# Bias rearranged by GpSimd into reading order, and all turned probabilities copied from PSUM by ScalarE

## The chip, the cores and the metric

One core of one Trainium2 chip runs the whole program in one launch. The metric is the device time of that launch in microseconds (us), as a median over runs. Five engines work beside each other and meet only at semaphores: TensorE (PE in the profile, with PEld for its weight loads), VectorE (DVE), ScalarE (ACT), GpSimd (POOL) and SyncE (SP), which mostly issues transfers. Each takes its instructions in order.

## What is computed

The reference is a small network over 1024 tokens (a grid of 16 rows and 64 columns) and 256 context tokens, all in float32, width 1024. Two hybrid layers (a short convolution, a retention branch and a neighbourhood attention branch side by side) are followed by a block with a recurrent mixer, a pooling mixer and a feed-forward part. Only the neighbourhood attention matters here. For each of 6 heads of width 64, a query at grid place (r, c) looks at a window of 8 rows by 16 columns around it and at all 256 context tokens:

```
s_loc = einsum(q, k_win) * scale + rpb[head, dr, dc]     # a bias for each offset in the window
s_ctx = einsum(q, k_ctx) * scale                         # no bias
p = softmax(concat([s_loc, s_ctx]))
o = p_loc @ v_win + p_ctx @ v_ctx
```

In the first of the two layers the 256 context tokens also attend among themselves; in the second they don't.

## The kernel before

Nearly all the work is in dense products: a weight slab of 128 output features is loaded by SP into one of two buffers `raw[0]`, `raw[1]`, GpSimd splits it into a high and a low part (`split`, L480 and L482), and TensorE runs three matmuls for each product (`slab`, L561). Slabs are numbered; `split_done`, `slab_done` and `evac_done` count them. In each layer the slabs of the neighbourhood projections come first, then the stretch of this case, the attention itself, and then the slabs of the convolution (numbers from `G_CONV` on). Of those, the first two slabs have been loaded before the attention begins, and the second is still being split when it begins.

**The attention.** The queries are arranged so that a tile is 8 grid columns by 16 rows (128 queries), tiles t = 0 to 7. A tile sees three tiles of keys (24 columns by 16 rows, 384 keys) and the 256 context keys, 640 in all; keys are stored column by column, so a key's place is 16 * column + row. Heads go in pairs (j = 0, 1, 2). A unit is a (j, t), done in the order of `NA_ORDER`, and in the first layer two units of context queries follow in each pair (256 keys only): 30 units in the first layer, 24 in the second. A unit has these steps:

- scores (`scores`, L828): TensorE makes 128 x 640 scores for each of the two heads into PSUM banks 0 to 3 (matmuls on L846, L850 for context units). It first waits for `nm_ready` of the unit before.
- maxima (`maxima`, L1817): for each head VectorE adds the bias to the scores, writes the sum to `Sb`, takes the row maximum (L1839, one custom instruction) and negates it (L1841), which gives `nm_ready`. `Sb` has two buffers for head 0 and one for head 1, so head 1 waits until TensorE has turned the head 1 of the unit before.
- exponentials (`exps`, L1326): ScalarE, on `Sb` in place, with the row sum (L1331).
- turning (`turn_keys`, L854): TensorE transposes ten tiles of 128 x 128 into PSUM banks 4 to 6 (L867), 4, 4 and 2 to a bank (a context unit has four tiles, one bank). Head 1 begins with the sixth tile and waits for the exponentials of head 1.
- copies out of PSUM (`turned`): ScalarE copies banks 4 and 6 (L1342), VectorE copies bank 5 (L1856), into the single buffer `PT`, so each waits until the products of the unit before have been made.
- products (`apply`, L871): 20 matmuls of turned probabilities and values (L884) and 4 that spread the inverse sums (L888). VectorE multiplies them into `Y` (`place`, L1869 and L1870).

The engines run ahead of each other by one unit. The orders that matter are:

```
PE : scores(i+1)  turn_keys(i)  apply(i-1)
ACT: exps(i+1, head 0)  turned(i)  exps(i+1, head 1)
DVE: maxima(i+1)  sums(i)  turned(i)  place(i-1)
```

**The bias.** In HBM the bias is laid out row by row: a key's place is 64 * row + column. For each pair of heads three bias tiles are loaded: one for the middle tiles (t = 1 to 6), one for t = 0 and one for t = 7. `load_bias` (L389) issues eight transfers for one of them. There are two slots; a slot is two heads of 128 x 1024, and slot 1 is `biasB0` and the weight buffer `raw[0]`. `biases` (L439) issues the loads from SP, each as soon as `nm_ready` says that a slot is free; the first one of a layer is issued from ScalarE. The bias is read through a view in which neighbouring elements are 64 words apart, since scores and bias have different orders. Context keys have no bias; VectorE clears that part of the slot (L1822, L1823) at each switch. Behind the last bias load SP goes on with the weight slabs.

GpSimd does nothing in the attention stretch, other than finishing the split of the second convolution slab: its next split waits for the first convolution slab.

Of the kernel before, what the change touches and what calls it, by code (L numbers as in the profile page):

```python
# [114 lines left out]
NA_ORDER = [1, 2, 0, 3, 4, 7, 5, 6]  # L115
# [48 lines left out]
def build_kernel(nc, xT, cT, modw, vecs, mats, ropes, rets, bias, s8, s4, s2, rgw, poolw, pooltab, pT, outT):  # L164
    V, A, T, G = nc.vector, nc.scalar, nc.tensor, nc.gpsimd
    with ExitStack() as ctx:
# [39 lines left out]
        biasA = at("biasA", W_CT, [P, 2, SEQ])  # L206
        biasB0 = at("biasB0", W_B + 2 * NEAR_KEYS, [P, SEQ])
# [36 lines left out]
        bias_slot = [[biasA[:, 0, :], biasA[:, 1, :]], [biasB0[:], raw[0][:]]]  # L244
# [61 lines left out]
        bias_in = [sem("bias_in0"), sem("bias_in1")]  # L306
        s_ready, nm_ready = sem("s_ready"), sem("nm_ready")
        p_ready, pt_ready, pt_dve, pt_act = sem("p_ready"), sem("pt_ready"), sem("pt_dve"), sem("pt_act")
# [25 lines left out]
        CUTS = (0, 14, LAYER_AT[1] + 14, G_RMIX)  # L334
# [36 lines left out]
        def bias_tile(t):  # L371

            return t if t in (0, QT - 1) else 1

# [4 lines left out]
        def bias_loads(l, slot):  # L379

            return [(m, j, t) for m in range(l + 1) for j in range(PAIRS) for t in (1, 0, QT - 1)
                    if bias_slot_of(j, t) == slot]

        def bias_count(l, j, t):

            slot = bias_slot_of(j, t)
            return 128 * (bias_loads(l, slot).index((l, j, bias_tile(t))) + 1)

        def load_bias(eng, l, j, t):  # L389

            slot = bias_slot_of(j, t)
            for x, nx in BIAS_ROWS:
                k0 = 2 * min(max(x - 2, 0), QT - KEYT) * GRID_W
                b = (PAIRS * l + j) * QT + x
                r = 2 * BLK_W * x
                for a in range(2):
                    src = bias[b:b + nx, :, a, :].rearrange("x (y q) n -> (x y) q n", y=2)
                    eng.dma_start(bias_slot[slot][a][r:r + 2 * BLK_W * nx, k0:k0 + LOC],
                                  src[:, BLK_W * t:BLK_W * (t + 1), :]).then_inc(bias_in[slot], 16)
# [24 lines left out]
        def _(sp):  # L424
# [14 lines left out]
            def biases(l):  # L439

                units, ub = na_units(l), na_base(l)
                for j in range(PAIRS):
                    if j == 0:
                        sp.wait_ge(bias_clear, 2 * l + 2)
                    else:
                        sp.wait_ge(nm_ready, 2 * (ub + j * na_tiles(l)))
                    load_bias(sp, l, j, 0)
                    sp.wait_ge(nm_ready, 2 * (ub + units.index((j, 0)) + 1))
                    load_bias(sp, l, j, QT - 1)
                    sp.wait_ge(nm_ready, 2 * (ub + units.index((j, QT - 1)) + 1))  # L450
                    if j + 1 < PAIRS:
                        load_bias(sp, l, j + 1, 1)
# [20 lines left out]
        def _(pool):  # L473
# [27 lines left out]

            for g0, turns, places in runs(CUTS):
                if g0 == 0:
# [12 lines left out]
                if g0 + 2 * turns in CUTS[1:3]:  # L516
                    weighted_queries(CUTS.index(g0 + 2 * turns) - 1)

# [12 lines left out]
        def _(pe):  # L531
# [102 lines left out]
            for l in range(2):  # L634
# [193 lines left out]
                def scores(i):  # L828

                    j, t = units[i]  # L830
                    if i:
                        if i == 1:
                            keep_busy(7, 4)
                        pe.wait_ge(nm_ready, 2 * (ub + i))
# [19 lines left out]
                def turn_keys(i):  # L854
# [3 lines left out]
                    ga, gd = groups_before(l, i, 0, 2), groups_before(l, i, 1, 2)  # L858
                    for x, (a, _, p) in enumerate(tiles):
# [4 lines left out]
                        if x == 4 and gd:  # L864
                            pe.wait_ge(pt_dve, gd)
# [5 lines left out]
                def apply(i):  # L871
# [4 lines left out]
                    pe.wait_ge(pt_act, groups_before(l, i + 1, 0, 2))  # L876
                    pe.wait_ge(pt_dve, groups_before(l, i + 1, 1, 2))
# [294 lines left out]
        def _(act):  # L1172
# [35 lines left out]
            for l in range(2):  # L1208
# [105 lines left out]
                act.wait_ge(bias_clear, 2 * l + 1)  # L1314
                load_bias(act, l, 0, 1)
# [18 lines left out]
                def turned(i):  # L1334

                    for g in range(0, turned_groups(units[i][1]), 2):
# [1077 lines left out]
```

## Time and profile before

| | us |
|---|---|
| median of 3 runs | 3225.45 |
| lowest and highest | 3223.82, 3229.87 |
| the profiled execution's own time | 3228.54 |
| its span in the trace | 3226.7 |
| attention stretch, first layer | from 477.6 to 610 |
| attention stretch, second layer | from 1257.6 to 1372.6 |

| engine | busy us | share of the span |
|---|---|---|
| PE | 3120.1 | 97% |
| DVE | 1511.6 | 47% |
| ACT | 730.4 | 23% |
| POOL | 1131.6 | 35% |

Times inside the trace count from the start of the span. A row of the timeline gives the start, the length, the engine, the line of the kernel, the operation, what it writes and reads, how many instructions are merged in it, and in brackets how long the engine stood idle before it and for whom it waited. The ends of matmuls are modelled.

### The profile page before, as it was taken

The page shows a single profiled execution, that of the slowest core. Times are in us where ns is not written, and L with a number is a line of the kernel's source. Part 1 is how long each engine was busy: PE and PEld are TensorE (multiplying, and loading weights), DVE is VectorE, ACT ScalarE, POOL GpSimd, SP SyncE. Part 2 cuts the span into 40 slices and gives each one's busy share as a digit, 9 for nine tenths or more (in the row PEclk, how much of TensorE's full clock was granted, in tenths as well). Part 3 has the DMA queues.
Part 4 walks back from the last instruction along what each step waited for, and adds up shares of the span by engine and source line. Part 5 has one row for each costly group of instructions (what it writes and reads, how often), then busy time and mean ns, then how long its engine had stood idle before and what let it go on. Part 6 is the DMA issues. An engine that isn't in the chain of part 4 may idle for free.

```text
span 3226.7 us, 41362 instructions
## 1 busy us (share of the span) xinstructions
PE 3120.1 (97%) x17382; PEld 2527.6 (78%) x17382; DVE 1511.6 (47%) x1647; ACT 730.4 (23%) x940; POOL 1131.6 (35%) x525
## 2 busy tenths in 40 slices
PE   6999998899999999899999999999899999999998
PEld 5877886787878787788577788788688888888877
DVE  3124508428733423824677601443664056155477
ACT  2011215312231122511245501122211001001132
POOL 2222230026643222034133444453244344443442
PEclk9999999999999999999999999999999999999999
DMA  6200011333231011112111111112211111111211
GB/s 238 78 27 14 33 43 44 112 117 134 66 128 40 10 45 40 60 40 98 72 46 46 40 53 50 39 53 98 78 52 46 52 46 48 50 46 52 106 44 72
DMA packets 60188, 206.07 MB, mean 64 GB/s; under 512 B 5904, under 2 KB 7696, under 8 KB 60048
## 3 DMA queue, kind: packets, MB, share of 16 engines
q1 hardware_dynamic: 42384, 143.15, 13.7%
q10 hardware_dynamic: 17664, 60.87, 5.0%
q8 instruction: 111, 1.82, 0.2%
q14 instruction: 29, 0.24, 0.0%
HBM read 187.22 MB, written 16.78 MB: 63 GB/s over the span
## 4 chain that ended last, share of the span: by engine, by line
PE 77%; DVE 10%; issue 7%; POOL 3%; DMA 2%; ACT 1%; ACTq 0%; POOLq 0%; DVEq 0%; SPq 0%
PE ps L561 66%; DVE Sb L1839 3%; PE ps L846 2%; POOL w_hi L480 1%; POOL w_lo L482 1%; DVE C L2070 1%; DMA raw<-s 1%; PE ps L1034 1%; DMA modfirst<-modw 1%; PE ps L756 1%; PE ps L671 1%; PE ps L536 1%; PE ps L589 1%; PE ps L1015 0%; PE ps L762 0%
## 5 line engine op out<-in xcount | busy, mean ns | idle before, releaser
L480 POOL TENSOR_TENSOR w_hi<-raw,pool_zero 128x1024 fp32r<-128x1024 f32 (+2 forms) x242 | 457.6, 1891 | 2000.8 <-PE ps L561 1826.9
L482 POOL TENSOR_TENSOR w_lo<-raw,w_hi 128x1024 fp32r<-128x1024 f32 (+2 forms) x242 | 639.1, 2641 | 19.0
L561 PE MATMUL ps<-h_hi,w_hi 128*128 128x512 f32 (+1 forms) x1808 | 481.9, 363 | 6.2 <-POOL w_lo L482 2.5
L561 PE MATMUL ps<-g_hi,w_hi 128*128 128x512 f32 x1488 | 465.9, 394 | 2.1 <-DVE g_lo L2151 1.5
L561 PE MATMUL ps<-h_hi,w_lo 128*128 128x512 f32 (+1 forms) x1808 | 461.9, 352 | 0.0
L561 PE MATMUL ps<-h_lo,w_hi 128*128 128x512 f32 (+1 forms) x1808 | 461.5, 351 | 0.0
L561 PE MATMUL ps<-g_lo,w_hi 128*128 128x512 f32 x1488 | 459.1, 390 | 0.0
L561 PE MATMUL ps<-g_hi,w_lo 128*128 128x512 f32 x1488 | 459.1, 390 | 0.0
L561 PEld LDWEIGHTS ps<-h_hi,w_hi 128*128 128x128 f32 x1808 | 296.4, 188 | 76.5 <-issue 24.3
L561 PEld LDWEIGHTS ps<-h_hi,w_lo 128*128 128x128 f32 x1808 | 293.7, 188 | 48.9
L561 PEld LDWEIGHTS ps<-g_hi,w_hi 128*128 128x128 f32 x1488 | 279.4, 189 | 67.2 <-issue 7.0
L561 PEld LDWEIGHTS ps<-h_lo,w_hi 128*128 128x128 f32 x1808 | 293.3, 188 | 47.9
L561 PEld LDWEIGHTS ps<-g_lo,w_hi 128*128 128x128 f32 x1488 | 279.9, 188 | 58.6
L561 PEld LDWEIGHTS ps<-g_hi,w_lo 128*128 128x128 f32 x1488 | 279.9, 188 | 58.5
L561 PE MATMUL ps<-r_hi,w_lo 128*128 128x512 f32 x576 | 177.4, 389 | 0.0
L561 PE MATMUL ps<-r_hi,w_hi 128*128 128x512 f32 x576 | 177.3, 389 | 0.0
L561 PE MATMUL ps<-r_lo,w_hi 128*128 128x512 f32 x576 | 177.2, 389 | 0.0
L2195 DVE TENSOR_TENSOR gpad<-ps,token_scale 128x1024 f32<-128x1024 f32 x24 | 29.4, 1225 | 209.3 <-PE ps L561 201.2
L561 PEld LDWEIGHTS ps<-r_hi,w_hi 128*128 128x128 f32 x576 | 108.1, 188 | 22.5
L561 PEld LDWEIGHTS ps<-r_hi,w_lo 128*128 128x128 f32 x576 | 108.1, 188 | 22.4
L561 PEld LDWEIGHTS ps<-r_lo,w_hi 128*128 128x128 f32 x576 | 108.1, 188 | 22.4
L1585 ACT ACTIVATE ffc<-ffc,vec 128x1024 f32<-128x1024 f32 x24 | 27.6, 1152 | 342.4 <-DVE ffc L2200 342.4
(333 smaller groups left out, 3529.6 us busy)
## 6 DMA issues: line engine op xcount, KB each, us to landing
raw<-s SPq DMA_DIRECT2D x226, 512.0 KB, 3.5
modring<-modw ACTq DMA_DIRECT2D x32, 512.0 KB, 4.6
x_saved<-Y ACTq DMA_DIRECT2D x2, 4096.0 KB, 12.8
modfirst<-modw SPq DMA_DIRECT2D x4, 1024.0 KB, 10.7
modfirst<-modw ACTq DMA_DIRECT2D x4, 1024.0 KB, 19.4
xin<-x_saved ACTq DMA_DIRECT2D x1, 4096.0 KB, 13.4
B<-x_saved ACTq DMA_DIRECT2D x1, 4096.0 KB, 15.5
x_saved<-B ACTq DMA_DIRECT2D x1, 4096.0 KB, 11.7
```

The lines of the kernel that those rows point to most:

```text
L480: G.tensor_tensor(w_hi[s][:, :n], raw[s][:, :n], zero.to_broadcast([P, n]), ALU.add).then_inc(hi_done, 1)
L482: G.tensor_tensor(w_lo[s][:, :n], raw[s][:, :n], w_hi[s][:, :n].bitcast(F32), ALU.subtract)\
L536: T.matmul(ps[:, bank * BANK:bank * BANK + 3 * P].rearrange("p (x f) -> p x f", f=P), ones, cm[:], start=True, stop=True)
L561: last = T.matmul(ps[:, o + c0:o + c0 + size], wt[s][:, kk], xx[:, k, t0:t0 + size], start=(x == 0 and n == 0), stop=(x == k_n - 1 and n = ...
L589: last = T.matmul(ps[:, o + c0:o + c0 + size], wt[s][:, k * P:(k + 1) * P], xx[:, k, t0:t0 + size], start=(k == 0 and n == 0), stop=(k == ...
L671: last = T.matmul(ps[:, (6 + half) * BANK:(7 + half) * BANK], ret_const[:, 0, :], QK[:, c, CTX + 512 * half:CTX + 512 * (half + 1)], start ...
L756: T.matmul(ps[r, c:c + P], ST[r, d, STATE_AT[d](n), :], qw[i % 2][r, d, t * P:(t + 1) * P], start=(t == 0 and x == 0), stop=False, skip_gr ...
L846: last = T.matmul(ps[:, o:o + size], QK[r, 3 + j, q0:q0 + P], QK[r, j, k0:k0 + size], start=True, stop=True)
L1034: last = T.matmul(ps[:, (4 + 2 * m) * BANK + c0:(4 + 2 * m) * BANK + c0 + size], rgwt[:, 8 * m + c, :], xcs[c % 2][:, t0:t0 + size], start ...
L1839: own.link(V.tensor_tensor_reduce(out=p, in0=s, in1=b, scale=1.0, scalar=MASKED, op0=ALU.add, op1=ALU.max, accum_out=m[:, a:a + 1]))
L2070: ins = V.tensor_tensor(total, total, C2[:, 8 + k, :] if sq is None else sq, ALU.add)
L2195: V.tensor_tensor(gpad[:, 2:], ps[:, b:b + SEQ], token_scale[:], ALU.mult).then_inc(evac_done, 1)
```

## The change

- The bias tiles are now kept in reading order (16 * column + row, 640 words a head), in two slots of their own (`biasA` with three parts, and `biasB0`). The transfers go into a staging area instead: the first of a layer into `PT0` and `bias_raw0`, the other eight all into the pair `raw[0]`, `raw[1]`.
- GpSimd rearranges each tile from the staging area into its slot (`set_bias`): for each head a memset of 256 words and a copy of 384 words whose source elements are 64 words apart. Nine in each layer. It waits for the transfer and for the slot, and counts `bias_set`. The first of a layer stands ahead of the split of the first convolution slab; behind the split of the second one GpSimd sets both raw buffers to the masked value (`stage_clear`), and then does the other eight.
- SP issues the next bias load when `bias_set` says that the staging area has been read; before, it waited for a slot.
- VectorE waits for `bias_set` and reads the bias in one run of 640 words. Its memsets of the context part are gone. It also clears other areas ahead of the stretch (`PT0` and `bias_raw0`, 2048 words, in place of 4096).
- TensorE's scores wait for `s_read` of both heads, which VectorE's L1839 instruction counts itself, and not for the negated maximum that follows it.
- VectorE's copy of bank 5 is gone. ScalarE makes three copies (4, 4 and 2 tiles), and TensorE waits for all three where it waited for two of ScalarE and one of VectorE.
- The order of the tiles puts t = 0 fifth (third before) and t = 7 seventh (sixth before).
- The loops over slabs of GpSimd are cut at two more places in each layer, for the new calls.

```diff
-NA_ORDER = [1, 2, 0, 3, 4, 7, 5, 6]
+NA_ORDER = [1, 2, 3, 4, 0, 5, 7, 6]
...
-        biasA = at("biasA", W_CT, [P, 2, SEQ])
-        biasB0 = at("biasB0", W_B + 2 * NEAR_KEYS, [P, SEQ])
+        biasA = at("biasA", W_CT, [P, 3, NEAR_KEYS])
+        biasB0 = at("biasB0", W_B + 2 * NEAR_KEYS, [P, NEAR_KEYS])
+        bias_raw0 = at("bias_raw0", W_B, [P, SEQ])
...
-        bias_slot = [[biasA[:, 0, :], biasA[:, 1, :]], [biasB0[:], raw[0][:]]]
+        bias_slot = [[biasA[:, 0, :], biasA[:, 1, :]], [biasA[:, 2, :], biasB0[:]]]
+        bias_raw = [[PT0[:], bias_raw0[:]], [raw[0][:], raw[1][:]]]
...
-        CUTS = (0, 14, LAYER_AT[1] + 14, G_RMIX)
+        CUTS = (0, 14, G_CONV, G_CONV + 2, LAYER_AT[1] + 14, LAYER_AT[1] + G_CONV, LAYER_AT[1] + G_CONV + 2, G_RMIX)
...
+        bias_order = [(j, t) for j in range(PAIRS) for t in (1, 0, QT - 1)]
...
-                units, ub = na_units(l), na_base(l)
-                for j in range(PAIRS):
-                    if j == 0:
-                        sp.wait_ge(bias_clear, 2 * l + 2)
+                for n, (j, t) in enumerate(bias_order[1:]):
+                    if n == 0:
+                        sp.wait_ge(stage_clear, l + 1)
                     else:
-                        sp.wait_ge(nm_ready, 2 * (ub + j * na_tiles(l)))
-                    load_bias(sp, l, j, 0)
-                    sp.wait_ge(nm_ready, 2 * (ub + units.index((j, 0)) + 1))
-                    load_bias(sp, l, j, QT - 1)
-                    sp.wait_ge(nm_ready, 2 * (ub + units.index((j, QT - 1)) + 1))
-                    if j + 1 < PAIRS:
-                        load_bias(sp, l, j + 1, 1)
+                        sp.wait_ge(bias_set, 9 * l + n + 1)
+                    load_bias(sp, l, j, t, 1, stage_in)
+                sp.wait_ge(bias_set, 9 * (l + 1))
...
+            def set_bias(l, n):
+
+                j, t = bias_order[n]
+                units, ub = na_units(l), na_base(l)
+                if n:
+                    pool.wait_ge(stage_in, 128 * (8 * l + n))
+                else:
+                    pool.wait_ge(stage_first, 128 * (l + 1))
+                if t == QT - 1:
+                    pool.wait_ge(nm_ready, 2 * (ub + units.index((j, 0)) + 1))
+                elif j and t:
+                    pool.wait_ge(nm_ready, 2 * (ub + units.index((j - 1, QT - 1)) + 1))
+                elif j:
+                    pool.wait_ge(nm_ready, 2 * (ub + j * na_tiles(l)))
+                slot = bias_slot_of(j, t)
+                c0 = ROW if t == QT - 1 else 0
+                k0, z0 = (CTX, 0) if t == QT - 1 else (0, NEAR_KEYS - CTX)
+                for a in range(2):
+                    b = bias_slot[slot][a]
+                    G.memset(b[:, z0:z0 + CTX], 0.0)
+                    last = G.tensor_copy(b[:, k0:k0 + NEAR_KEYS - CTX].rearrange("p (c r) -> p c r", r=ROWS),
+                                         bias_raw[1 if n else 0][a].rearrange("p (r c) -> p c r", c=GRID_W)[:, c0:c0 + ROW_LOC, :])
+                last.then_inc(bias_set, 1)
+
             for g0, turns, places in runs(CUTS):
+                for l in range(2):
+                    if g0 == LAYER_AT[l] + G_CONV:
+                        set_bias(l, 0)
+                    if g0 == LAYER_AT[l] + G_CONV + 2:
+                        pool.wait_ge(split_done, g0)
+                        G.memset(raw[0][:], MASKED)
+                        G.memset(raw[1][:], MASKED).then_inc(stage_clear, 1)
+                        for n in range(1, 9):
+                            set_bias(l, n)
...
-                        pe.wait_ge(nm_ready, 2 * (ub + i))
+                        pe.wait_ge(s_read, 2 * (ub + i))
...
-                    ga, gd = groups_before(l, i, 0, 2), groups_before(l, i, 1, 2)
+                    ga = groups_before(l, i, 0, 1)
                     for x, (a, _, p) in enumerate(tiles):
                         if x == 0 or a != tiles[x - 1][0]:
                             pe.wait_ge(p_ready, 2 * (ub + i) + a + 1)
                         if x == 0 and ga:
                             pe.wait_ge(pt_act, ga)
-                        if x == 4 and gd:
-                            pe.wait_ge(pt_dve, gd)
...
-                    pe.wait_ge(pt_act, groups_before(l, i + 1, 0, 2))
-                    pe.wait_ge(pt_dve, groups_before(l, i + 1, 1, 2))
+                    pe.wait_ge(pt_act, groups_before(l, i + 1, 0, 1))
...
-                act.wait_ge(bias_clear, 2 * l + 1)
-                load_bias(act, l, 0, 1)
+                act.wait_ge(bias_clear, l + 1)
+                load_bias(act, l, 0, 1, 0, stage_first)
...
-                    for g in range(0, turned_groups(units[i][1]), 2):
-                        n = 4 if g == 0 else 2
+                    for g in range(turned_groups(units[i][1])):
+                        n = 2 if g == 2 else 4
...
-                V.memset(biasA[:], MASKED).then_inc(bias_clear, 1)
-                V.memset(biasB0[:], MASKED)
-                dve.wait_ge(split_done, g0 + G_CONV + 1)
-                V.memset(raw[0][:], MASKED).then_inc(bias_clear, 1)
+                V.memset(PT0[:], MASKED)
+                V.memset(bias_raw0[:], MASKED).then_inc(bias_clear, 1)
                 units, ub = na_units(l), na_base(l)
-
-                def zeros(j, t, a):
-
-                    return bias_slot[bias_slot_of(j, t)][a].rearrange("p (r c) -> p r c", c=GRID_W)[:, :, ROW_LOC:ROW]
 
                 def maxima(i):
 
                     j, t = units[i]
                     if t in (0, 1, QT - 1):
-                        dve.wait_ge(bias_in[bias_slot_of(j, t)], bias_count(l, j, t))
-                        V.memset(zeros(j, t, 0), 0.0)
-                        own.link(V.memset(zeros(j, t, 1), 0.0))
+                        dve.wait_ge(bias_set, 9 * l + bias_order.index((j, t)) + 1)
                     dve.wait_ge(s_ready, ub + i + 1)
                     m = st[:, i % 2, :]
                     for a in range(2):
@@ -1829,15 +1836,12 @@
                         elif i >= 2:
                             dve.wait_ge(pt_ready, groups_before(l, i - 1, 0, 1))
                         size, o = NEAR_KEYS if t < QT else CTX, 2 * a * BANK
-                        if t < QT:
-                            c0 = ROW_LOC if t == QT - 1 else 0
-                            b = bias_slot[bias_slot_of(j, t)][a].rearrange("p (r c) -> p c r", c=GRID_W)[:, c0:c0 + ROW, :]
-                        else:
-                            b = zeros(j, 1, a)
-                        p, s = [x.rearrange("p (c r) -> p c r", r=ROWS) for x in (probabilities(i, a)[:, :size],
-                                                                                  ps[:, o:o + size])]
-                        own.link(V.tensor_tensor_reduce(out=p, in0=s, in1=b, scale=1.0, scalar=MASKED, op0=ALU.add,
-                                                        op1=ALU.max, accum_out=m[:, a:a + 1]))
+                        b = bias_slot[bias_slot_of(j, t if t < QT else 1)][a]
+                        b = b if t < QT else b[:, NEAR_KEYS - CTX:]
+                        p, s = probabilities(i, a)[:, :size], ps[:, o:o + size]
+                        V.tensor_tensor_reduce(out=p, in0=s, in1=b, scale=1.0, scalar=MASKED, op0=ALU.add,
+                                               op1=ALU.max, accum_out=m[:, a:a + 1]).then_inc(s_read, 1)
+                        dve.wait_ge(s_read, 2 * (ub + i) + a + 1)
                         V.tensor_scalar(m[:, 2 + a:3 + a], m[:, a:a + 1], -1.0, None, ALU.mult).then_inc(nm_ready, 1)
 
                 def sums(i):
@@ -1846,14 +1850,6 @@
                     if i >= 2:
                         dve.wait_ge(pv_ready, ub + i - 1)
                     V.reciprocal(st[:, i % 2, 6:8], st[:, i % 2, 4:6]).then_inc(rinv_ready, 1)
-
-                def turned(i):
-
-                    if units[i][1] < QT:
-                        dve.wait_ge(pt_ready, groups_before(l, i, 0, 1) + 2)
-                        if ub + i:
-                            dve.wait_ge(pv_ready, ub + i)
-                        V.tensor_copy(turned_tile(4, 4), ps[:, 5 * BANK:6 * BANK]).then_inc(pt_dve, 1)
 
...
-                    turned(i)
```

## Rows read from the trace of the kernel before

**Rows 1.** The page, part 4: shares of the chain that ended last, by line.

```profile
PE ps L561 66%; DVE Sb L1839 3%; PE ps L846 2%; POOL w_hi L480 1%; POOL w_lo L482 1%; DVE C L2070 1%; DMA raw<-s 1%; PE ps L1034 1%; DMA modfirst<-modw 1%; PE ps L756 1%; PE ps L671 1%; PE ps L536 1%; PE ps L589 1%; PE ps L1015 0%; PE ps L762 0%
```

**Rows 2.** Timeline, VectorE: head 0 of units 1, 27 (first layer), 1, 23 (second).

```profile
483.46 1.27 DVE L1839 CUSTOM_DVE_ANT_1 Sb<-ps,biasA 128x640 f32<-128x640 f32 x1 [1.46 <-PE ps L846]
...
595.43 1.28 DVE L1839 CUSTOM_DVE_ANT_1 Sb<-ps,biasA 128x640 f32<-128x640 f32 x1 [0.22 <-PE ps L846]
...
1263.47 1.27 DVE L1839 CUSTOM_DVE_ANT_1 Sb<-ps,biasA 128x640 f32<-128x640 f32 x1 [1.46 <-PE ps L846]
...
1362.18 1.26 DVE L1839 CUSTOM_DVE_ANT_1 Sb<-ps,biasA 128x640 f32<-128x640 f32 x1 [0.22 <-PE ps L846]
```

**Rows 3.** Timeline of one unit in the first layer.

```profile
494.90 0.87 ACT L1342 ACTIVATE PT<-ps 128x512 f32<-128x512 f32 x2 [0.34 <-PE ps L888]
...
495.04 1.36 PE L846 MATMUL ps<-QK 64*128 64x384 f32 x12 [0.25 <-DVE st L1841]
...
495.65 0.83 ACT L1331 ACTIVATE Sb<-Sb,st 128x640 f32<-128x640 f32 x1
...
496.33 1.31 PE L867 MATMUL ps<-cm,Sb 128*128 128x128 f32 x10
...
496.45 1.27 DVE L1839 CUSTOM_DVE_ANT_1 Sb<-ps,biasA 128x640 f32<-128x640 f32 x1 [0.22 <-PE ps L846]
...
497.58 1.31 PE L884 MATMUL ps<-PT,Vt 128*64 128x128 f32 x20
...
497.83 1.28 DVE L1839 CUSTOM_DVE_ANT_1 Sb<-ps,biasA 128x640 f32<-128x640 f32 x1
...
498.72 0.39 PE L888 MATMUL ps<-cm,st 128*64 128x128 f32 x4
...
499.34 0.69 DVE L1856 COPY PT<-ps 128x512 f32<-128x512 f32 x1
...
499.37 1.35 PE L846 MATMUL ps<-QK 64*128 64x256 f32 x12 [0.26 <-DVE st L1841]
```

**Rows 4.** Timeline, end of the second layer's stretch: units without new scores.

```profile
1364.94 0.87 ACT L1342 ACTIVATE PT<-ps 128x512 f32<-128x512 f32 x2 [0.34 <-PE ps L888]
...
1365.70 0.83 ACT L1331 ACTIVATE Sb<-Sb,st 128x640 f32<-128x640 f32 x1
...
1366.67 0.53 PEld L867 LDWEIGHTS ps<-cm,Sb 128*128 128x128 f32 x5 [0.21 <-ACT Sb L1331]
...
1367.37 1.31 PE L884 MATMUL ps<-PT,Vt 128*64 128x128 f32 x20
...
1368.51 0.39 PE L888 MATMUL ps<-cm,st 128*64 128x128 f32 x4
...
1369.00 0.87 ACT L1342 ACTIVATE PT<-ps 128x512 f32<-128x512 f32 x2 [2.38 <-PE ps L888]
```

**Rows 5.** Groups by form, ScalarE, 477.6 to 610: copies of turned probabilities.

```profile
L1342 ACT ACTIVATE PT<-ps 128x512 f32<-128x512 f32 x30 | 17.8, 592 | 13.5 <-PE ps L888 13.5
...
L1342 ACT ACTIVATE PT<-ps 128x256 f32<-128x256 f32 x24 | 9.0, 377 | 0.0
```

**Rows 6.** Groups by form, VectorE, 477.6 to 610: bias, scores and maximum.

```profile
L1839 DVE CUSTOM_DVE_ANT_1 Sb<-ps,biasA 128x640 f32<-128x640 f32 x28 | 35.5, 1270 | 14.9 <-PE ps L846 14.7 <-DVE biasA L1823 0.2
...
L1839 DVE CUSTOM_DVE_ANT_1 Sb<-ps,biasA 128x256 f32<-128x256 f32 x8 | 3.4, 420 | 1.6 <-PE ps L867 1.3
```

**Rows 7.** Timelines, SyncE and VectorE, first layer: a bias load and its first reader.

```profile
575.89 0.71 SPq L398 DMA_DIRECT2D biasB<-bias  x1
...
586.22 0.27 DVE L1822 MEMSET biasB<- 128x256 f32 x1 [0.46 <-DMA raw<-bias]
```

**Rows 8.** GpSimd: timeline at the second stretch's start; then groups by form.

```profile
1258.58 2.36 POOL L482 TENSOR_TENSOR w_lo<-raw,w_hi 128x1024 fp32r<-128x1024 f32 x1
...
L480 POOL TENSOR_TENSOR w_hi<-raw,pool_zero 128x1024 fp32r<-128x1024 f32 x226 | 442.7, 1959 | 1918.5 <-PE ps L561 1744.6 <-PE ps L589 149.9 <-DMA raw<-s 24.0
...
L498 POOL TENSOR_TENSOR qw<-QK,WQ 128x384 f32<-128x384 f32 x12 | 11.7, 1000 | 17.2 <-PE ps L762 17.2
```

More of the change, by code:

```diff
@@ L304, in build_kernel @@
                                                             sem("hn_var"), sem("hn_std"), sem("hn_done"))
-        bias_in = [sem("bias_in0"), sem("bias_in1")]
-        s_ready, nm_ready = sem("s_ready"), sem("nm_ready")
-        p_ready, pt_ready, pt_dve, pt_act = sem("p_ready"), sem("pt_ready"), sem("pt_dve"), sem("pt_act")
+        stage_first, stage_in, stage_clear, bias_set = sem("stage_first"), sem("stage_in"), sem("stage_clear"), sem("bias_set")
+        s_ready, s_read, nm_ready = sem("s_ready"), sem("s_read"), sem("nm_ready")
+        p_ready, pt_ready, pt_act = sem("p_ready"), sem("pt_ready"), sem("pt_act")
         rinv_ready, pv_ready, y_used = sem("rinv_ready"), sem("pv_ready"), sem("y_used")
@@ L369, in groups_before, with load_bias @@
             return sum(len(range(first, turned_groups(t), step)) for _, t in done)
-        def bias_tile(t):
-            return t if t in (0, QT - 1) else 1
         def bias_slot_of(j, t):
             return (j + (t in (0, QT - 1))) % 2
[L379 to L391, printed above, removed]
+        bias_order = [(j, t) for j in range(PAIRS) for t in (1, 0, QT - 1)]
+        def load_bias(eng, l, j, t, place, landed):
             for x, nx in BIAS_ROWS:
@@ L397, in load_bias @@
                     src = bias[b:b + nx, :, a, :].rearrange("x (y q) n -> (x y) q n", y=2)
-                    eng.dma_start(bias_slot[slot][a][r:r + 2 * BLK_W * nx, k0:k0 + LOC],
-                                  src[:, BLK_W * t:BLK_W * (t + 1), :]).then_inc(bias_in[slot], 16)
+                    eng.dma_start(bias_raw[place][a][r:r + 2 * BLK_W * nx, k0:k0 + LOC],
+                                  src[:, BLK_W * t:BLK_W * (t + 1), :]).then_inc(landed, 16)
         def probabilities(i, a):
@@ L515, in _ @@
                         split(x % 2, k, g)
-                if g0 + 2 * turns in CUTS[1:3]:
-                    weighted_queries(CUTS.index(g0 + 2 * turns) - 1)
+                for l in range(2):
+                    if g0 + 2 * turns == LAYER_AT[l] + 14:
+                        weighted_queries(l)
         FULL = [(0, 0, 512), (512, 512, 512), (1024, 1024, 256)]
```

## The prediction, made before the changed kernel was run

> **What bounds the kernel now.** I read the chain of waits first: two thirds of it are TensorE's slab matmuls (L561), which the change leaves alone [rows 1]. The share that can move lies in the two attention stretches (L1839, L846). So I read those as a pipeline with one period a unit. From head 0 of unit 1 to head 0 of unit 23 the second layer takes 98.7 us for 22 steps, 4.49 a unit; the first takes 112.0 for 26, which at 4.49 for its 20 steps between local units leaves 3.7 for each of the 6 around context units [rows 2].
>
> One unit in detail [rows 3]: scores start at 495.04 and again at 499.37, a period of 4.33. VectorE's sums for head 0 start 1.41 after the scores (496.45), head 1's at 497.83, and the next scores follow 1.54 later. This is a closed ring: scores, two sums, scores. TensorE stands idle in it for only 0.26, so its own work is 4.07 a unit. The rest of the 4.49 is switches of the bias. ScalarE has room.
>
> **Each part of the change.**
>
> *VectorE's sum.* The strided bias is the likely price of the long form: 640 elements take 1.270 us, and 256, whose bias comes in short runs of neighbours, take 0.420 [rows 6]. Per element that is 1.98 and 1.64 ns with all fixed cost in it. No row has 640 in reading order. Below it is bounded by VectorE's copy of 512 out of PSUM, 0.69 [rows 3], above by today's 1.27; I take 0.82, on the line through 0.420 for 256 and 0.69 for 512. Two sums save 0.9 of the ring. `s_read` in place of `nm_ready` saves another 0.15 (the negation). The copy (0.69) and the memsets (0.27 each, as in [rows 7], 18 of each head) leave VectorE as well. So this ring falls to about 3.3 and is no longer what binds.
>
> *ScalarE's third copy.* The two copies start at 494.90 and the exponential of head 1, queued behind them, at 495.65 [rows 3]. Two take 0.87 together, one of 256 takes 0.377 [rows 5], so a copy of 512 holds the queue for 0.50. Now the ring that this lengthens: `turned(i)`, then head 1 of `exps(i+1)`, then the second half of `turn_keys(i+1)`, then `apply(i)`, and only then `turned(i+1)`, because `PT` has one buffer. At the end of the second stretch no scores stand between and the ring can be seen bare [rows 4]: copies at 1364.94, exponential 1365.70 (+0.76), second half of the turning 1366.67 (+0.97, released by the exponential), products 1367.37 (+0.70), inverse sums 1368.51 (+1.14), next copies 1369.00 (+0.49). That is 4.06. Today it hides under 4.33. With one more copy of 512 it is **4.56**, above TensorE's 4.07 and above today's period. The scores fit inside it: they start behind the inverse sums and take 1.29 (495.04 to 496.33), while the turning can't start before the third copy ends, some 1.5 after the first began.
>
> Against 4.49 this adds 0.07 a step: 22 steps give +1.6 in the second layer, 20 give +1.5 in the first (steps around context units have as many short copies as before: +0). The first scores of each layer come 1.0 sooner behind two short sums (-1.0 each). The last two rounds have a third copy each, with nothing to absorb it: +1.0 in the second layer, +0.5 in the first, where context units end it.
>
> *The bias through one staging area.* This is what I think costs most. Loads and rearrangements now alternate, since SP waits for `bias_set` and GpSimd for the load. A load takes 10.3 from its first issue (575.89) to the reader that waited for it (586.22) [rows 7]; two other waits of this kind give 10.2 and 10.8. A rearrangement is 2 memsets of 256 and 2 strided copies of 384. GpSimd has no such row. The nearest is its two-input product of 384 at 1.00 [rows 8]; I take 1.0 for the copy (one input less, but strided) and 0.3 for the memset (VectorE's takes 0.27), so 2.7 with a hand-over. Below: 0.55 and 0.27, VectorE's speed, 1.6 in all. Above: 1.5 and 0.5, 4.0. So one bias needs 10.3 + 2.7 + 0.1 = 13.1. Eight follow each other, and a pair of heads needs three, 39.3, while it lasts 8 x 4.56 = 36.5 in the second layer. The staging falls behind.
>
> In the second layer: the split ends at 1260.94 [rows 8], two memsets of 1024 (1.1 each; at most 1.96 as the split's first half) clear the staging at 1263.1, so biases n = 1 to 8 are set at 1276.2 + 13.1(n - 1). Units need them (units 4, 6, 8, 12, 14, 16, 20, 22) at 1262.5 + 4.56(k - 1). Late by: 0, 4.0, 8.0, 2.8, 6.8, 10.8, 5.7, 9.6. The largest counts once: 10.8. Some is absorbed: head 0 could start 1.2 after the copies and is needed by ScalarE 1.3 later than it comes, head 1 must let the scores go 1.1 later; take 1.1. Delay 9.7. Sum of the second layer: -1.0 + 1.6 + 9.7 + 1.0 = **+11.3**.
>
> In the first layer I take the split to end as far ahead of unit 1 (2.5). Bias 2 is set at 509.3, unit 6 wants it at 505.3: 4.0 less 1.1 is 2.9. After that a pair lasts 7 x 4.56 + 3 x 3.7 = 43.0, longer than 39.3, so nothing more. Sum: -1.0 + 1.5 + 2.9 + 0.5 = **+3.9**.
>
> *What costs nothing.* The first `set_bias` of a layer (2.7) stands where GpSimd waits some 7 us or more for TensorE in each round of splits. Weight slabs behind the last bias load: bias 8 is set at 1367.9 or later, the stretch ends near 1384, and the first convolution slab, already split, runs before they are wanted; if GpSimd were 10 us later still, this cover would be gone. VectorE's clearing is shorter than before.
>
> The page "GPSIMD Engine Reference" of the Trainium skill, Engine selection, says of GpSimd that one-input work is roughly line-rate, which would make 384 elements an estimated 0.3 us and the sum about +5. The same page's Performance pitfalls says that a read step over 8 bytes costs about 2.9 cycles an element, an estimated 0.9; no row here shows either.
>
> **Sum.** +11.3 + 3.9 = +15.2. The profiled execution took 3228.5, so it would take 3243.7; the median before is 3225.45, 3.1 lower, and on it I forecast **3241**.
>
> **Rivals.**
>
> A, the forecast (ring of 4.56 and staging of 13.1): 3241, chance 0.48.
>
> B, GpSimd slow (4.0 a bias, memsets of 1.96): staging 14.4; bias 8 is set at 1380.0 against 1358.3, delay 20.6, the second layer +22.2; the first waits 7.2 to 7.5, +8.5. Together +31: 3256, 0.15. Strided reads speak for it, no row against it.
>
> C, GpSimd fast (1.6 a bias): staging 12.0; the largest lateness is 4.5, less 1.1 is 3.4; second layer +5.0, first +1.5. +6.5: 3232, 0.12. The nearest row speaks against it. The line rate of the Trainium skill (page "GPSIMD Engine Reference", Engine selection) would lie here or lower.
>
> D, the third copy doesn't lengthen the period (4.33 stays), staging decides: unit 22 wants its bias at 1353.4, it comes at 1367.9, delay 13.4; second layer -1.0 - 3.4 + 13.4 = +9.0, first -1.0 - 3.2 + 4.0 = -0.2. +9: 3234, 0.11. Against it: the bare ring of [rows 4].
>
> E, **faster**: the copy is hidden, TensorE's 4.07 binds, and GpSimd takes 1.6. Then bias 8 (1358.9) is 10.9 later than unit 22 wants it (1348.0), delay 9.8; second layer -1.0 - 9.2 + 9.8 = -0.4, first -1.0 - 8.4 + 2.9 = -6.5. -7: 3218.5, 0.07. It decides from the point where copies, exponential, half turning and products fit in 4.07; ScalarE copies 512 in 0.592 where VectorE needs 0.69 [rows 3, 5], which speaks for it. "Advanced Engine Details and Errata" of the Trainium skill, TRN2 Errata, says the same, that ScalarE is closer to PSUM; by that rule alone the move is a gain.
>
> F, the change doesn't do what it says, sums stay at 1.27: head 1 then holds the scores back by 0.06 a unit, the first scores gain nothing, most of it vanishes under the staging. +17: 3242.5, 0.07.
>
> **How the numbers follow.** A measurement of this kernel tells about 0.2%, 6.5 us, from no change. Slower by more: A, B, D, F and half of C, 0.87, of which I give 0.05 to what I haven't seen: 0.82. Faster: E, 0.07. The rest, 0.11, is the same. The range leaves out E and the upper half of B: 3230 to 3258.
>
> **What would show it.** A period of 4.56 between units that wait for no bias, and ScalarE's three copies starting 0.50 apart, right behind L888. The second half of the turning released by ScalarE. VectorE's long form near 0.82. VectorE idle for GpSimd's copy at units 6, 8 and 16 of the second layer, about 3, 4 and 3 us, and once in the first. SP's loads 13 apart. If the waits for GpSimd are missing, the staging step is wrong; if the period is 4.1, the ring is; if GpSimd's copy takes 2 us, B it is.

## The result and the profile after

The changed kernel takes 3233.09 us (median of 9 runs) against 3225.45 before (the median of 9 runs too): 7.6 us slower, ratio 1.0021 with a 95% interval of 1.0012 to 1.0029. One of the nine, at a mean granted clock of 0.749, took 3926 us and is left out of the ratio. The direction is as forecast and the time lies in the range, but the increase is half of the 15.2 that the forecast added up.

In the trace the loss lies where it was expected, in the two attention stretches, from the first scores to the first matmul of the convolution slabs. Timeline of TensorE after the change, both ends of both stretches:

```profile
476.89 1.36 PE L864 MATMUL ps<-QK 64*128 64x384 f32 x12 [1.33 <-ACT Y L1194]
...
610.90 0.50 PE L579 MATMUL ps<-h_hi,w_hi 128*128 128x512 f32 x1 [0.71 <-DVE Y L1866]
...
1258.08 0.59 PE L864 MATMUL ps<-QK 64*128 64x384 f32 x2 [1.11 <-ACT Y L1194]
...
1378.49 0.38 PE L579 MATMUL ps<-h_hi,w_hi 128*128 128x256 f32 x1 [0.72 <-DVE Y L1866]
```

That is 134.0 and 120.4; before, the same ends stood at 477.63 and 610.45 (132.8) and 1257.64 and 1372.61 (115.0). So +1.2 and +5.4, 6.6 in all. The spans of the two profiled executions differ by only 4.6 (3231.3 and 3226.7): outside the stretches the second execution took 2.0 less. So a few us between medians or spans say less than the stretches do.

One unit of the first layer after the change, timeline (answers to [rows 3], and with its ring laid open to [rows 4]):

```profile
497.90 1.36 ACT L1357 ACTIVATE PT<-ps 128x512 f32<-128x512 f32 x3 [1.25 <-PE ps L903]
...
499.13 0.82 DVE L1842 CUSTOM_DVE_ANT_0 Sb<-ps,biasA 128x640 f32<-128x640 f32 x1 [0.67 <-PE ps L864]
499.13 0.84 ACT L1346 ACTIVATE Sb<-Sb,st 128x640 f32<-128x640 f32 x1
...
499.40 1.48 PE L883 MATMUL ps<-cm,Sb 128*128 128x128 f32 x10 [0.32 <-ACT PT L1357]
...
500.11 0.53 PEld L883 LDWEIGHTS ps<-cm,Sb 128*128 128x128 f32 x5 [0.21 <-ACT Sb L1346]
...
500.81 1.31 PE L899 MATMUL ps<-PT,Vt 128*64 128x128 f32 x20
...
501.95 0.39 PE L903 MATMUL ps<-cm,st 128*64 128x128 f32 x4
...
502.45 1.36 ACT L1357 ACTIVATE PT<-ps 128x512 f32<-128x512 f32 x3 [1.34 <-PE ps L903]
```

The three copies start at 497.90 and again at 502.45: a period of 4.55, where 4.56 had been worked out. Each link is there: the start of the three copies, then head 1's exponential (+1.23), the second half of the turning released by it (+0.98), products (+0.70), inverse sums (+1.14), copies (+0.50). TensorE, which stood idle 0.26 a unit before, now waits for the copies (0.32), and its weight loads for the exponential (0.21). VectorE's sum has the price that was forecast, and VectorE waits for TensorE (0.67) instead of setting the pace. Its group by form in the first stretch, which answers to [rows 6]:

```profile
L1842 DVE CUSTOM_DVE_ANT_0 Sb<-ps,biasA 128x640 f32<-128x640 f32 x38 | 31.3, 824 | 111.4 <-PE ps L864 100.9 <-PE ps L883 7.2 <-POOL biasB L506 3.4
```

824 ns against 1270 before: reading the bias in one run is worth 0.45 a sum.

The staging, GpSimd and SyncE in the first layer (answers to [rows 7] and to the unknown price beside [rows 8]):

```profile
492.17 0.31 POOL L505 MEMSET biasA<- 128x256 f32 x1 [9.87 <-DMA raw<-bias]
492.43 0.85 POOL L506 COPY biasA<-raw 128x384 f32<-128x384 f32 x1
...
493.47 0.86 POOL L506 COPY biasB<-raw 128x384 f32<-128x384 f32 x1
...
494.36 5.78 SPq L387 DMA_DIRECT2D raw<-bias  x8
...
504.18 0.31 POOL L505 MEMSET biasA<- 128x256 f32 x1 [9.85 <-DMA raw<-bias]
```

A rearrangement takes 2.2 (492.17 to 494.33) and not 2.7, a load 9.8 (494.36 to 504.18) and not 10.3. From one bias to the next it is 12.0, in place of 13.1. The next two views are the places where VectorE waits for it in the second layer, the sums of head 0 for units 6 to 10, and the granted clock of TensorE in windows around them (columns as on the page: window, PE, PEld, DVE, ACT, POOL busy, clock, transfers):

```profile
1287.16 0.82 DVE L1842 CUSTOM_DVE_ANT_0 Sb<-ps,biasA 128x640 f32<-128x640 f32 x1 [2.98 <-POOL biasB L506]
...
1290.39 0.82 DVE L1842 CUSTOM_DVE_ANT_0 Sb<-ps,biasA 128x640 f32<-128x640 f32 x1 [0.67 <-PE ps L864]
...
1298.76 0.82 DVE L1842 CUSTOM_DVE_ANT_0 Sb<-ps,biasA 128x640 f32<-128x640 f32 x1 [4.63 <-POOL biasB L506]
...
1301.99 0.82 DVE L1842 CUSTOM_DVE_ANT_0 Sb<-ps,biasA 128x640 f32<-128x640 f32 x1 [0.67 <-PE ps L864]
...
1307.76 0.82 DVE L1842 CUSTOM_DVE_ANT_0 Sb<-ps,biasA 128x640 f32<-128x640 f32 x1 [0.67 <-PE ps L864]
```

```profile
1295.00:1300.00 5.00, 2.94 (x34) 2.35 (x34) 1.20 (x4) 0.93 (x3) 2.13 (x4) 1.00 0.04 15
1300.00:1303.00 3.00, 2.23 (x16) 1.81 (x17) 2.23 (x9) 2.79 (x7) 0.00 (x0) 0.83 0.30 86
1303.00:1306.00 3.00, 3.00 (x28) 2.67 (x28) 1.09 (x5) 0.92 (x2) 0.00 (x0) 0.60 0.23 81
```

Three things are to be seen. Units 6 and 8 wait for GpSimd, as forecast, by 3.0 and 4.6 (in the first layer unit 6 does, by 3.4). The unit behind each wait follows after 3.23, not 4.55: 1.3 of it is made good at once. And behind the longer wait, in which TensorE stood idle for 2.6, its granted clock, 1.00 before (2.4 GHz), has means of 0.83 and 0.60 in the next two windows, so for a part of them it was at 1.2 GHz, and one unit took 5.77, 1.2 more than 4.55.

### The profile page after: what moved, and what is told of

Same layout as the page of the kernel before. It is cut to its first block, busy times and chain, and to the rows that moved or that the text cites. A ratio compares the mean times of both kernels' runs of the same rounds, so it can differ in the third digit from the quotient of the medians.

```text
span 3231.3 us, 41364 instructions
## 1 busy us (share of the span) xinstructions
PE 3126.9 (97%) x17382; PEld 2526.9 (78%) x17382; DVE 1435.1 (44%) x1561; ACT 753.7 (23%) x988; POOL 1173.3 (36%) x601
## 4 chain that ended last, share of the span: by engine, by line
PE 78%; issue 7%; DVE 6%; POOL 4%; DMA 2%; ACT 2%; SPq 1%; ACTq 0%; POOLq 0%; DVEq 0%
PE ps L579 66%; POOL w_hi L464 2%; POOL w_lo L466 1%; PE ps L883 1%; ACT PT L1357 1%; PE ps L899 1%; DVE C L2065 1%; PE ps L1049 1%; DMA raw<-s 1%; DMA modfirst<-modw 1%; PE ps L774 1%; PE ps L689 1%; SPq L387 1%; PE ps L554 1%; DMA raw<-bias 1%
## 5 line engine op out<-in xcount | busy, mean ns | idle before, releaser
L1842 DVE CUSTOM_DVE_ANT_0 Sb<-ps,biasA 128x640 f32<-128x640 f32 (+1 forms) x86 | 66.9, 778 | 222.9 <-PE ps L864 189.2
## 6 DMA issues: line engine op xcount, KB each, us to landing
xin<-x_saved ACTq DMA_DIRECT2D x1, 4096.0 KB, 12.8
```

The lines of the kernel that those rows point to most:

```text
L1842: V.tensor_tensor_reduce(out=p, in0=s, in1=b, scale=1.0, scalar=MASKED, op0=ALU.add, op1=ALU.max, accum_out=m[:, a:a + 1]).then_inc(s_read, 1)
```

## Experiments

The theory: (1) the third copy lengthens the ring to 4.55, and (2) the staging makes units wait in both layers. The rival to the first is that the copy is hidden and all of the loss is staging. Lengths of the two stretches, read in each trace from the same two rows as above:

| kernel | first | second | both, against before | median us | ratio to before (95%) |
|---|---|---|---|---|---|
| before | 132.8 | 115.0 | | 3225.45 | |
| changed | 134.0 | 120.4 | +6.6 | 3233.09 | 1.0021 (1.0012 to 1.0029) |
| copy_back | 125.0 | 115.6 | -7.3 | 3221.2 | 0.9986 (0.9977 to 0.9995) |
| direct | 133.1 | 115.7 | +1.1 | 3230.32 | 1.0011 (1.0002 to 1.0021) |
| both | 121.6 | 105.1 | -21.1 | 3205.65 | 0.9945 (0.9931 to 0.9958) |
| only_copies | 138.7 | 116.7 | +7.6 | 3233.1 | 1.0018 (1.0009 to 1.0027) |
| slow_set | 138.0 | 125.4 | +15.6 | 3242.17 | 1.0048 (1.0034 to 1.0062) |
| exp_first | 138.0 | 120.9 | +11.1 | 3239.66 | 1.0041 (1.0027 to 1.0055) |
| old_order | 143.0 | 124.5 | +19.7 | 3247.58 | 1.006 (1.0046 to 1.0074) |

The kernel before and the changed one were measured in a first batch, the others in two later ones, beside which the kernel before had medians of 3225.99 (first four) and 3226.39 (last three).

**copy_back.** The changed kernel, with VectorE's copy of bank 5 again.

```diff
-                    for g in range(turned_groups(units[i][1])):
-                        n = 2 if g == 2 else 4
+                    for g in range(0, turned_groups(units[i][1]), 2):
+                        n = 4 if g == 0 else 2
...
+                        V.tensor_copy(turned_tile(4, 4), ps[:, 5 * BANK:6 * BANK]).then_inc(pt_dve, 1)
```

> The changed kernel with one part undone: VectorE copies bank 5 of the turned probabilities again, ScalarE copies banks 4 and 6. Theory 1 (the third copy lengthens the ring of copies, exponential of head 1, turning, products to 4.55 us): a unit that waits for nothing takes about 4.1, TensorE's own 4.07; the first layer's stretch gets 8 us shorter than in the changed kernel, the second, where GpSimd and the transfers now set the pace (12.0 a bias, 36 for a pair against 32.8), only 5. Total near 3220, 5 below the kernel before. Theory 2 (the third copy is hidden and all of the loss is waiting for the staged bias): the period stays near 4.5 and the time near 3233.

Measured: 3221.2, and stretches 9.0 and 4.8 shorter than the changed kernel's, against 8 and 5 expected. The sums of head 0 in VectorE's timeline, units 11 and 15 of the second layer, and the waits in that layer:

```profile
1302.67 0.82 DVE L1845 CUSTOM_DVE_ANT_0 Sb<-ps,biasA 128x640 f32<-128x640 f32 x1
...
1318.93 0.83 DVE L1845 CUSTOM_DVE_ANT_0 Sb<-ps,biasA 128x640 f32<-128x640 f32 x1
```

```profile
POOL biasA L505 <- DMA raw<-bias: 79.4, 8, 10.4
...
DVE Sb L1845 <- POOL biasB L506: 10.1, 4, 4.5
DVE Sb L1845 <- POOL biasA L506: 2.7, 1, 2.7
```

Four units take 16.26 here, 4.07 each, and VectorE now waits for GpSimd five times in the second layer, 12.8 in all, where the changed kernel waited 8.5 (the two waits above and 0.9 at unit 16): the faster the units, the more the staging binds. Beside the staging the third copy costs about 12 us (3233.1 against 3221.2), so the theory that it is hidden falls. Without it the rest of the change gains some 5 us.

**direct.** No staging: the host lays the three tiles of a pair out in reading order, with their zeros (layout only, as it did before in another order), and SyncE brings each into its slot when `nm_ready` has freed it.

```diff
-            for x, nx in BIAS_ROWS:
...
+            for a in range(2):
+                eng.dma_start(bias_slot[slot][a], bias[n, :, a, :]).then_inc(bias_in[slot], 16)
...
-                        for n in range(1, 9):
-                            set_bias(l, n)
```

> The changed kernel with the staging gone: the host lays out the three bias tiles of a pair in reading order with the zeros of the context keys, two transfers bring one straight into its slot, GpSimd takes no part, ScalarE still makes three copies. Theory 1: the period stays 4.55, the waits of VectorE for GpSimd (3.4 in the first layer, 7.6 in the second, of which a good 1 each is absorbed) go: about 6 to 7 us less than the changed kernel, near 3226.5, the same as before. Theory 2 (staging alone costs): it falls to 4.1 a unit and to 3208.

Measured: by the stretches 0.9 and 4.7 below the changed kernel, 5.6 in all, a little less than the 6 to 7 expected. The median of 3230.3 is only 2.8 lower, and 4 above the 3226.5 expected; the profiled execution took 3227.3, 3 below that median. So the size lies between 2.8 and 5.6, and what the difference is isn't settled. VectorE, head 0 of units 7 and 11 of the second layer:

```profile
1284.73 0.82 DVE L1811 CUSTOM_DVE_ANT_0 Sb<-ps,biasA 128x640 f32<-128x640 f32 x1 [0.67 <-PE ps L834]
...
1302.95 0.82 DVE L1811 CUSTOM_DVE_ANT_0 Sb<-ps,biasA 128x640 f32<-128x640 f32 x1 [0.67 <-PE ps L834]
```

The period is still 4.55 (18.22 for four units) with no staging at all, which is what theory 1 says and theory 2 of this run (4.1) doesn't.

**both.** The two edits together: of the change only the bias in reading order in slots of its own (without VectorE's memsets for it), the new release of the scores and the tile order are left. These are not told apart by any run.

> Staging gone and bank 5 back on VectorE, so that only the bias in reading order remains of the change. Theory 1: neither ring binds, TensorE's own work does, 4.07 to 4.1 a unit for 42 steps between local units: 22 x (4.49 - 4.1) + 20 x 0.39 = 16 below the kernel before and a little more for switches: 3208. Rival: something else near 4.33 binds (the wait of head 1 for the turning of the unit before), and it is near 3219.

Measured: 3205.65, 20 us and 0.55% below the kernel before, a little more than expected. VectorE, head 0 of three units in the second layer, and a window of four units (columns as above):

```profile
1300.67 0.82 DVE L1814 CUSTOM_DVE_ANT_0 Sb<-ps,biasA 128x640 f32<-128x640 f32 x1
...
1304.65 0.82 DVE L1814 CUSTOM_DVE_ANT_0 Sb<-ps,biasA 128x640 f32<-128x640 f32 x1
...
1308.81 0.82 DVE L1814 CUSTOM_DVE_ANT_0 Sb<-ps,biasA 128x640 f32<-128x640 f32 x1
...
1292.55:1308.81 16.26, 16.26 (x186) 13.19 (x185) 12.98 (x41) 10.40 (x25) 0.00 (x0) 1.00 0.31 91
```

Two units in 8.14, 4.07 each, which is TensorE's own work in [rows 3], and TensorE is busy for all of the 16.26 of the window. Nothing else binds here. This is the version to keep.

The four kernels with the new sum show that the two costs overlap. The third copy costs 24.7 without the staging (direct against both) and 11.9 with it; the staging costs 15.6 without the third copy (copy_back against both) and 2.8 with it (the changed kernel against direct). A slower unit asks for its bias later, and VectorE's waits for GpSimd fit this: 17.6 in copy_back, 11.9 in the changed kernel. Neither price can be read from one experiment alone.

**only_copies.** The kernel before with `turned` as in the change and nothing else.

> The kernel before with one part of the change: ScalarE makes all three copies, the bias and everything else as before (strided sums of 1.27 us). Theory 1: 4.55 a unit in place of 4.33, but the switches of the bias, 0.5 each, now hide below it: +0.07 to +0.15 for 42 steps and 1.5 at the ends: +4.5 to +8, 3230 to 3233. Theory 2 (the third copy is hidden, VectorE is relieved of 0.69): 4.33 stays or less, 3220 to 3225.

Measured: 3233.1, the upper end of theory 1. VectorE, head 0 of two units in the first layer:

```profile
505.58 1.28 DVE L1836 CUSTOM_DVE_ANT_1 Sb<-ps,biasA 128x640 f32<-128x640 f32 x1 [0.86 <-PE ps L846]
...
510.14 1.29 DVE L1836 CUSTOM_DVE_ANT_1 Sb<-ps,biasA 128x640 f32<-128x640 f32 x1 [0.86 <-PE ps L846]
```

4.56 a unit, with VectorE relieved of its 0.69 and idle for 0.86 where it was idle for 0.22. Moving the copy alone is a loss, and the same ring shows it with the strided sums of before. (The profiled execution was 5 us above its median. TensorE's granted clock had a mean of 0.66 from 570 to 575, where one unit took 5.31, and of 0.94 and 0.50 in the windows from 610 and from 615. So 138.7 is too long for this kernel, by 1 to 2 us; the rest of the 5 isn't explained.)

**slow_set.** The changed kernel with its staging slowed to what the forecast had assumed.

```diff
+                    G.memset(b[:, k0:k0 + NEAR_KEYS - CTX], 0.0).then_inc(extra, 1)
+                    pool.wait_ge(extra, 2 * (9 * l + n) + a + 1)
                     G.memset(b[:, z0:z0 + CTX], 0.0)
```

> The changed kernel, with one more memset of 384 words and a wait for it ahead of each half of a rearrangement, which puts a bias near 13.1 us in place of 12.0: the value that I had forecast. If the size of the staging was what the forecast had wrong, this kernel gives the forecast's sum: bias 6 of the second layer comes 6 x 1.05 later, that layer +6.3, the first one +2.1 (bias 2), 8 above the changed kernel, 3241. If the error lay elsewhere (slack, ends, early units), it gives 3237 or less.

Measured: 3242.17, 9.1 above the changed kernel. From one bias to the next it now takes 13.0:

```profile
1277.07 0.42 POOL L505 MEMSET biasA<- 128x384 f32 x1 [10.50 <-DMA raw<-bias]
...
1367.83 0.42 POOL L505 MEMSET biasA<- 128x384 f32 x1 [9.61 <-DMA raw<-bias]
```

Seven steps in 90.8. With the forecast's input the kernel gives nearly the forecast's output, 3242 for 3241, and by stretch +5.2 and +10.4 for +3.9 and +11.3. So the size of this step is what separates 15 from 7. That the sum comes out within 1 us is partly luck: windows of this trace hold 13.6 us at half clock (6.8 in each layer) where those of the changed kernel hold 3.4, a cost that the forecast didn't have. One us in a step that eight biases go through one after the other costs 9 us.

**exp_first.** The kernel direct, with ScalarE's order turned round.

```diff
-                    turned(i)
                     if i + 1 < len(units):
                         exps(i + 1, 1)
+                    turned(i)
```

> The kernel without staging and with three copies by ScalarE, in which ScalarE makes the exponential of head 1 ahead of the copies and not behind them. If the ring is what I say, taking the exponential out of it doesn't help, because the sum of head 1 waits for the turning of the unit before and the copies now wait for it: turning, sum of head 1 (1.2), exponential (0.95), copies (1.5): about 4.7 a unit in place of 4.55, +6 us, 3236. If ScalarE's order is of no account, the time stays near 3230.

Measured: 3239.66, 9.3 above direct (10.0 by the stretches), where 6 was expected. Head 0 of units 4 and 6 of the second layer starts at 1278.51 and 1287.88 and of unit 20 at 1353.45: 74.9 for 16 units, 4.68 a unit, as worked out (4.7). That gives 5.5 for 42 steps. Of the rest, 3 lie in the units behind the start of a stretch or, in the first layer, of a pair (unit 3 of the second layer takes 5.14 for direct's 4.11) and 1.4 behind the last sums; why isn't settled. The order that the kernel has is the better one.

**old_order.** The changed kernel with the tile order of before.

> The changed kernel with the tile order of before, so that the staged biases are wanted at units 2 and 5 of the first pair, not at 4 and 6. Bias 1 is set at 1275.3 in the second layer, unit 2 wants it at 1267: 7 us of delay in place of 4 to 5 in the second layer and 2 in the first: about 6 us above the changed kernel, 3239. If the order is of no account, 3233.

Measured: 3247.58, 14.5 above the changed kernel, where 6 was expected. The wait stands where it was expected, at unit 2, but it costs more. VectorE, units 1 and 2 of the first layer, windows behind them, and TensorE's turning of one unit:

```profile
482.37 0.82 DVE L1842 CUSTOM_DVE_ANT_0 Sb<-ps,biasA 128x640 f32<-128x640 f32 x1 [1.99 <-PE ps L864]
...
494.51 0.82 DVE L1842 CUSTOM_DVE_ANT_0 Sb<-ps,biasA 128x640 f32<-128x640 f32 x1 [9.81 <-POOL biasB L506]
```

```profile
490.00:495.00 5.00, 0.00 (x0) 0.00 (x0) 0.49 (x1) 0.00 (x0) 2.09 (x4) 0.68 0.06 23
495.00:500.00 5.00, 3.67 (x18) 2.85 (x19) 2.92 (x12) 3.03 (x8) 0.00 (x0) 0.50 0.18 57
500.00:505.00 5.00, 4.67 (x45) 3.75 (x44) 2.27 (x7) 2.69 (x6) 0.55 (x2) 0.80 0.20 74
```

```profile
498.76 2.39 PE L883 MATMUL ps<-cm,Sb 128*128 128x128 f32 x10
```

TensorE does nothing in the window from 490 to 495, and its granted clock is at half from within it until after 500; turning takes 2.39 where it takes 1.48. So the new tile order is a part of the change that pays for itself, given the staging: it moves the first use of bias 1 from unit 2 to unit 4.

## Why the prediction was right and where it was wrong

The terms of the forecast's sum against the stretches, each stretch cut at head 0 of its unit 1 and of its last local unit (27 and 23), in us against the kernel before:

| | forecast | changed | direct |
|---|---|---|---|
| first layer, up to unit 1 | -1.0 | -0.35 | -0.35 |
| first layer, steps and waits | +1.5 and +2.9 | 0.0 | -0.9 |
| first layer, end | +0.5 | +1.5 | +1.5 |
| second layer, up to unit 1 | -1.0 | -0.4 | -0.35 |
| second layer, steps and waits | +1.6 and +9.7 | +4.7 | 0.0 |
| second layer, end | +1.0 | +1.1 | +1.1 |
| sum | +15.2 | +6.6 | +1.1 |

*What binds before.* The ring of scores and sums at 4.33 with TensorE's 4.07 below it: both shows TensorE's 4.07 once that ring is gone. Right.

*VectorE's sum, 0.82.* Measured 0.824. Right, and right too that it gains nothing while another ring is longer: with three copies and no staging (direct) the stretches are where they were.

*The third copy, 4.56.* Measured 4.55, and 4.56 with the old sums (only_copies). As a period it is right to the last link. But the forecast put it into all 42 steps between local units, +3.1, and direct, which has this ring and no staging, shows -0.9 and 0.0: behind the start of a stretch, and behind the context units, it isn't reached yet (in the second layer of direct units 2 and 3 follow after 3.53 and 4.11, in the first layer the units behind the context units after 3.23, 3.53 and 4.36). This term is 4.0 too high. What the copy costs depends on what else binds: 24.7 where nothing does (direct against both), 11.9 beside the staging (the changed kernel against copy_back), 7 beside the old sums (only_copies against before).

*The first scores 1.0 sooner.* From the first scores to the first sum of unit 1 it was 5.83 before (477.63 to 483.46) and is 5.48 now (476.89 to 482.37): 0.35. The filler matmuls that TensorE runs ahead of the scores of unit 1 (`keep_busy(7, 4)`, 478.18 to 480.96) now hold them back, which I hadn't counted. The end of the first layer costs 1.5 where I put 0.5.

*The staging, 13.1.* **This is the term that was mis-sized.** It is 12.0: the copy of 384 takes 0.85 where I put 1.0, from a two-input row; the two heads follow each other without a gap; the load takes 9.8 where I put 10.3. The mechanism was right (units 6 and 8, and a wait of 0.9 at unit 16 of the second layer; unit 6 of the first). But the delay is a small difference of two long rows of steps: with 12.0 in place of 13.1, and nothing else changed in the forecast's own working, the largest lateness is that of unit 8, 4.7 less 1.1, so 3.6 in place of 9.7, and in the first layer 1.8 less 1.1, 0.7 in place of 2.9. Measured, as changed less direct, the waits cost 4.7 and 0.9, and 1.2 of the 4.7 is the unit of 5.77 at the lower clock. slow_set, which puts the 13 back, makes 3242. With 12.0 the forecast's sum would be +6.9, near the 6.6 of the stretches, and there luck helps: the steps are 4.0 too high in it, the starts and ends together 2.4 too low and the waits 1.3.

*The slack of 1.1.* Measured 1.3 (3.23 in place of 4.55 behind a wait).

*The rivals.* The nearest number was rival C's, 3232, with a staging of 12.0. Its 12.0 was made of a rearrangement of 1.6 and a load of 10.3, where 2.2 and 9.8 were measured: the sum is right because the two errors cancel. D and E fall with the period of 4.55, F with the sum of 0.82, and B with a copy of 0.85.

The estimate of 0.9 for a strided copy of 384, worked out from the page "GPSIMD Engine Reference" of the Trainium skill, Performance pitfalls, was nearer to the 0.85 of the trace than the 1.0 from my row. The same page's line rate (Engine selection), an estimated 0.3, doesn't hold for this copy. With "Advanced Engine Details and Errata" of the Trainium skill, TRN2 Errata, which puts ScalarE closer to PSUM, the measured copies agree, 0.59 on ScalarE and 0.69 on VectorE; but the move was a loss, because it was ScalarE's place in the ring that counted and not the price of the copy.

## What to carry to other kernels

Before moving work to the engine that is less busy, follow what is queued behind it and close the ring: here ScalarE was busy for 56% of the first stretch before the change (72.5 of 130.4 us), and 0.50 more on it lengthened the period, since its copies stood between two steps of TensorE. And where a buffer is filled, rearranged and read in turns, multiply its step by the number of turns before comparing it with the work beside it: 1 us in the step was 9 us in the end. Data that is reordered on the chip in every run can be laid out so once, on the host: here the staging cost 15.6 us in the version where nothing hid it.

## What the runs showed of the hardware that wasn't expected

A wait for a buffer can be paid for twice, the second time by the granted clock. Behind the TensorE idle of 2.6 us in the changed kernel the windows above hold 3.4 us at half clock (twice the length of a window times what its mean lacks to 1.00: 2 x 3 x 0.17 and 2 x 3 x 0.40), and the timeline has the turning of that unit at 2.37 where it takes 1.48:

```profile
1300.58 1.36 PE L864 MATMUL ps<-QK 64*128 64x384 f32 x12 [2.56 <-DVE st L1842]
1302.13 2.37 PE L883 MATMUL ps<-cm,Sb 128*128 128x128 f32 x10 [0.19 <-ACT PT L1357]
```

Behind the first-layer wait of old_order the windows hold 10.2. VectorE's waits for GpSimd there add up to 20.9 against 11.9 in the changed kernel, 9.0 more, and the time is 14.5 more. But the length of the idle time doesn't decide it alone. In copy_back TensorE stood idle for 3.16 and went on at full clock; in only_copies the clock fell behind an idle of 1.62, with no long wait for a bias near it. TensorE's scores behind the idle time, copy_back and then only_copies, and the windows there:

```profile
1279.86 1.36 PE L864 MATMUL ps<-QK 64*128 64x384 f32 x12 [3.16 <-DVE st L1845]
...
1280.00:1285.00 5.00, 5.00 (x58) 4.02 (x58) 4.19 (x14) 3.48 (x10) 0.00 (x0) 1.00 0.25 87
```

```profile
569.81 2.38 PE L846 MATMUL ps<-QK 64*128 64x384 f32 x12 [1.62 <-DVE st L1838]
...
570.00:575.00 5.00, 4.84 (x34) 3.61 (x32) 2.69 (x6) 1.69 (x5) 0.00 (x0) 0.66 0.21 69
```

What decides it isn't shown by these runs. VectorE's sums weren't slowed by GpSimd's copies beside them: they take 0.82 to 0.83 with a copy running all the while (1321.42 in the changed kernel) and 0.82 without any (both).
